# Projection of layer 0 of a gated DeltaNet and RG-LRU backbone: two of five blocks of sums of squares and transposes moved behind a tile's fifth block

## The chip, the cores and the metric

The kernel runs on one core of one Trainium2 chip. The metric is the device time of one execution in microseconds; smaller is better. Times within one execution come from one profiled execution.

## The reference

Two layers over a latent stream of 2048 tokens and a prefix of 256 context tokens, 1024 wide, everything in float32. Layer 0 mixes with a bidirectional gated DeltaNet, layer 1 with a bidirectional RG-LRU. What matters here is the head of layer 0:

```python
proj = h @ w_in                                   # 1024 x 6208
qkv, z, ab = jnp.split(proj, [GDN_QKV_W, GDN_QKV_W + GDN_V_W], axis=-1)
qkv = jax.nn.silu(short_conv(qkv, conv_w))        # 4 taps over time
q, k, v = jnp.split(qkv, [GDN_QK_W, 2 * GDN_QK_W], axis=-1)
q = l2norm(q) * (GDN_HEAD_DIM ** -0.5)            # per head of 128
k = l2norm(k)
g = -jnp.exp(a_log) * jax.nn.softplus(ab[..., 0, :] + dt_bias)
# later: decay = exp(cumsum(g)[c] - cumsum(g)[s]) for each chunk of tokens
```

There are 8 heads of q and k and 16 of v and z, 128 wide each.

## The kernel before

The program runs phases one after another: modulation, norm, gates, the projection of layer 0 (`phase_project_gdn`), the delta core, the output, and then the same kind of phases for layer 1. The change touches `phase_project_gdn` alone.

**Heads, tiles, blocks.** The phase loops over `NQ` = 8 heads h. A head has `NT` = 6 tiles of 128 output features, in the order Q, Z0, K, Z1, V0, V1. A tile is computed for 2304 tokens in `NB` = 5 blocks: one of 256 (block 0) and four of 512 tokens (blocks 1 to 4). Each block is 24 matmuls into its own PSUM bank, `pj_bank` (L565): 8 slices of the contraction by three products of high and low parts. A stage is one tile on each of the engines. Stage (h, j) of each engine is written out by hand in program order, and the engines meet only at semaphores. Head 0 is written out, heads 1 to 7 run in a hardware loop (SyncE and GpSimd have their last head written out too).

**What happens to a tile.** ScalarE copies each bank into `pj_raw` (`take`, L837; with SiLU for Z0 and Z1). For q, k and v VectorE convolves the row (`conv`, L947 and L951) into `pj_acc`, once all five blocks have been taken. There is one `pj_raw`, so the take of the next tile's block 0 waits for the convolution, or for the store of z. One stage later ScalarE applies SiLU into `pj_row` (L853).

- For q and k it squares the row into `pj_acc` (L857). TensorE sums the squares over the features with a matrix of ones (`norms`, L785), ScalarE takes the root of each block (`root`, L865), and VectorE takes the reciprocal of the row (L933) and multiplies (L935, `normalise`). SyncE stores the row (`store_fm`, L657).
- k and v are transposed by TensorE (`turn`, L801), 4 chunks of 128 tokens to a bank, copied by ScalarE into `pj_tm` (`collect`, L877) and stored (`store_tm`, L664).

So five of the six stages have a **group** on TensorE: Q the transposes of the last V1 (trV1), Z0 the sums for q, Z1 the sums for k, V0 the transposes of k (trK), V1 those of V0 (trV0). K has none. A group has five blocks, b = 0 to 4, in three PSUM banks, `aux[b % 3]`: block 3 may be written once ScalarE has read block 0, and block 4 once it has read block 1 (the semaphore `aux_read`). The group stands behind block 3 of the tile, so behind the fourth of its blocks:

```python
for blk in range(NB):
    pr.products(pe, h, j, blk, first)
    if blk != 3:
        continue
    ...
```

**Decays.** Beside that, each stage makes three chunks of decays, o = 0 to 2, with two buffers. SyncE loads a chunk (L677, L679), ScalarE takes the absolute difference (L885) and the exponential (L888), GpSimd multiplies (L751, L754, L755), and SyncE stores the result (L688) and, once that has landed, loads the chunk after next into the buffer. ScalarE's order in a stage is decay 0, take 0 and 1, SiLU and square of the row before, decay 1, take 2 and 3, the group's roots or copies, decay 2, take 4.

**SyncE's queue.** In a stage SyncE issues, in this order: the next tile's weights (L539), store_tm or the store of z (L650), the store and the load of the last stage's decay 2, those of decay 0, in K and V0 store_fm, which waits for `norm`, and those of decay 1. It issues nothing else meanwhile.

Of the kernel before, what the change touches and what calls it, by code (L numbers as in the profile page):

```python
# [42 lines left out]
NQ = 8  # L43
# [3 lines left out]
NB = len(BLKS)  # L47
# [535 lines left out]
def phase_project_gdn(nc, sem, T, io, dram, hi, lo):  # L583
# [3 lines left out]
    Q, Z0, K, Z1, V0, V1 = range(6)  # L587
# [6 lines left out]
    with ExitStack() as ctx:  # L594
# [27 lines left out]
            return h * sum(k in kinds for k in KINDS) + sum(k in kinds for k in KINDS[:j + 1])  # L622

        PT = NCH // NT

        def item(h, j, o):

# [11 lines left out]
        with nc.Block() as block:  # L639
# [133 lines left out]

            @block.tensor
            def _(pe):
                def norms(h, j):

                    pe.wait_ge(s["square"], nth(h, j, "qk"))
                    base = aux_before(h, "ssQ" if j == Q else "ssK")
                    for b, (at, n) in enumerate(BLKS):  # L780
                        if b >= 3:
                            pe.wait_ge(s["aux_read"], base + b - 2)
                        elif b == 0 and not (isinstance(h, int) and h == 0 and j == Q):
                            pe.wait_ge(s["aux_read"], base)
                        pe.matmul(aux[b % 3][:, 0:n], T["ones"][:], acc[:, at:at + n], start=True, stop=True  # L785
                                  ).then_inc(s["aux"], 1)

                def turn(h, j, use):

                    if j == K:  # L790
                        pe.wait_ge(s["norm"], nth(h, j, "qk"))
                    else:
                        pe.wait_ge(s["silu"], nth(h, j, "qkv"))
                    base = aux_before(h, use)
                    for b in range(NB):
                        if b >= 3:
                            pe.wait_ge(s["aux_read"], base + b - 2)
                        elif b == 0:
                            pe.wait_ge(s["aux_read"], base)
                        for c in range(TRB * b, min(TRB * b + TRB, NCH)):  # L800
                            i = pe.transpose(aux[b % 3][:, (c % TRB) * P:(c % TRB + 1) * P],  # L801
                                             act_row[:, c * P:(c + 1) * P], T["ident"][:])
                        i.then_inc(s["aux"], 1)

                def stage(h, j, first):
                    for blk in range(NB):
                        pr.products(pe, h, j, blk, first)
                        if blk != 3:
                            continue
                        if j == Q and not first:  # L810
                            turn(h - 1, V1, "trV1")
                        if j == Z0:
                            norms(h, Q)
                        if j == Z1:
                            norms(h, K)
                        if j == V0:
                            turn(h, K, "trK")
                        if j == V1:
                            turn(h, V0, "trV0")
                sweep(pe, stage)  # L820
                turn(NQ - 1, V1, "trV1")

            @block.scalar
            def _(act):
                def take(h, j, blk, first):

                    act.wait_ge(pr.s_mm, (h * NT + j) * NB + blk + 1)
                    if blk == 0:
                        if first:
                            act.wait_ge(s["pads"], 1)  # L830
                        elif KINDS[j - 1] == "z":
                            act.wait_ge(s["z_out"], 32 * nth(h, j - 1, "z"))
                        elif j == 0:
                            act.wait_ge(s["conv"], nth(h, j, "qkv") - 1)
                        else:
                            act.wait_ge(s["conv"], nth(h, j - 1, "qkv"))
                    act.activation(raw_row(raw, blk), pr.bank[blk][:, 0:BLKS[blk][1]],  # L837
                                   ACT.Silu if KINDS[j] == "z" else ACT.Copy).then_inc(pr.s_ev, 1)

                def silu(h, j):  # L840
                    act.wait_ge(s["conv"], nth(h, j, "qkv"))
                    if j == Q:
                        if not (isinstance(h, int) and h == 0):
                            act.wait_ge(s["aux"], aux_before(h, "ssQ"))
                    elif j == K:
                        act.wait_ge(s["fm_out"], 16 * nth(h, Q, "qk"))
                    elif j == V0:
                        act.wait_ge(s["fm_out"], 16 * nth(h, K, "qk"))
                        act.wait_ge(s["aux"], aux_before(h, "trK") + NB)
                    else:  # L850
                        act.wait_ge(s["aux"], aux_before(h, "trV0") + NB)
                    for dst, src in zip((act_row[:, 0:CTX], act_row[:, CTX:TOK]), sequences(acc)):
                        i = act.activation(dst, src, ACT.Silu)  # L853
                    i.then_inc(s["silu"], 1)
                    if KINDS[j] in "qk":
                        act.wait_ge(s["silu"], nth(h, j, "qkv"))
                        act.activation(acc[:, 0:TOK], act_row[:], ACT.Square).then_inc(s["square"], 1)  # L857

                def root(h, j):

                    base = aux_before(h, "ssQ" if j == Q else "ssK")
                    q = KINDS[j] == "q"
                    for b, (at, n) in enumerate(BLKS):
                        act.wait_ge(s["aux"], base + b + 1)
                        act.activation(acc[:, at:at + n], aux[b % 3][:, 0:n], ACT.Sqrt,  # L865
                                       bias=epsq[:] if q else T["eps"][:], scale=float(HD) if q else 1.0
                                       ).then_inc(s["aux_read"], 1)

                def collect(h, j, use):

                    base = aux_before(h, use)
                    if not (isinstance(h, int) and h == 0 and j == K):
                        act.wait_ge(s["tm_out"], 16 * nth(h, j, "kv") - 16)
                    for b in range(NB):
                        n = min(TRB, NCH - TRB * b)
                        act.wait_ge(s["aux"], base + b + 1)
                        act.activation(tm[:, TRB * b:TRB * b + n].rearrange("p c t -> p (c t)"),  # L877
                                       aux[b % 3][:, 0:n * P], ACT.Copy).then_inc(s["aux_read"], 1)

                def decay(h, j, o):  # L880
                    c, b, k, u = item(h, j, o)
                    act.wait_ge(d_load[b], u * 48 + 48)
                    for dr in range(2):
                        for v in range(2):
                            i = act.activation(E[b][:, dr, v], E[b][:, dr, v], ACT.Abs, scale=-1.0, bias=gi[b][:, dr, Q_CG, v:v + 1])  # L885
                    i.then_inc(s["d_abs"], 1)
                    act.wait_ge(s["d_abs"], k + 1)
                    act.activation(E[b][:], E[b][:], ACT.Exp, scale=-1.0).then_inc(s["d_exp"], 1)  # L888

                def stage(h, j, first):  # L890
                    decay(h, j, 0)
                    take(h, j, 0, first)
                    take(h, j, 1, first)
                    if j == Q and not first:
                        silu(h - 1, V1)
                    if j == Z0:
                        silu(h, Q)
                    if j == Z1:
                        silu(h, K)
                    if j == V1:  # L900
                        silu(h, V0)
                    decay(h, j, 1)
                    take(h, j, 2, first)
                    take(h, j, 3, first)
                    if j == Q and not first:
                        collect(h - 1, V1, "trV1")
                    if j == Z0:
                        root(h, Q)
                    if j == Z1:
                        root(h, K)  # L910
                    if j == V0:
                        collect(h, K, "trK")
                    if j == V1:
                        collect(h, V0, "trV0")
                    decay(h, j, 2)
                    take(h, j, 4, first)
                sweep(act, stage)
                silu(NQ - 1, V1)
                collect(NQ - 1, V1, "trV1")

            @block.vector
            def _(dve):
# [1348 lines left out]
```

## Time and profile before

| | |
|---|---|
| Median of 3 runs | 4664.9 us (4652.61 to 4669.88) |
| Profiled execution | 4631.9 us, span 4630.1 us |
| TensorE (PE) matmul, busy | 4124.7 us, 89% of the span |
| TensorE weight loads (PEld) | 3436.1 us, 74% |
| VectorE (DVE) | 2331.1 us, 50% |
| ScalarE (ACT) | 2280.2 us, 49% |
| GpSimd (POOL) | 2017.1 us, 44% |
| Projection of layer 0, first to last L565 matmul | from 244.1 to 1645.9 us of the span |

Busy times are sums over the span and overlap. Matmuls are pipelined, and their ends are modelled. "[2.98 <-ACT pj_acc L865]" behind a row means that the engine stood idle for 2.98 us before it, and that the wait ended with the named work. SPq is SyncE's DMA queue; the row of a DMA lasts as long as its issue, not as long as the transfer. The projection's stages start where the first matmul of a tile's block 0 stands on TensorE.

### The profile page before, as it was taken

What the parts mean: (1) busy time and instruction counts of PE and PEld (TensorE: products, weight loads), DVE (VectorE), ACT (ScalarE), POOL (GpSimd) and SP (SyncE); (2) the same over time, 40 slices, a digit from 0 to 9 for tenths busy, and PEclk for the clock granted to TensorE, in tenths of its full rate; (3) what the DMA queues carried; (4) which work ended last, traced back from release to release, by engine and by line L of the source; (5) the groups of instructions that cost most, each with busy time, mean ns of one, the idle gap of its engine ahead of it and who ended that gap; (6) DMA issues with size and microseconds to landing.
All of it is one profiled execution on the core that took longest, in us unless ns stands there. A gap on an engine that the chain in (4) does not pass through costs nothing. (4 is left out here: it accounts for less than half of the span.)

```text
span 4630.1 us, 85462 instructions
## 1 busy us (share of the span) xinstructions
PE 4124.7 (89%) x30756; PEld 3436.1 (74%) x30756; DVE 2331.1 (50%) x2947; ACT 2280.2 (49%) x4473; POOL 2017.1 (44%) x1524
## 2 busy tenths in 40 slices
PE   6689999999999969999999999995999599977869
PEld 2377777777777758888888888884888488866657
DVE  3234444433433446666666666655554423338853
ACT  4245555555555546666666666652111511138832
POOL 2255455455555547666666666653111412100022
PEclk8799999999999989999999999997999699988889
DMA  6245545544544556666666666645444322254244
GB/s 227 91 122 150 150 142 151 152 139 144 151 144 143 158 170 197 182 193 190 192 179 193 188 184 188 183 137 204 177 181 154 100 100 104 110 225 180 80 141 136
DMA packets 775776, 733.27 MB, mean 158 GB/s; under 512 B 111808, under 2 KB 702656, under 8 KB 758272
## 3 DMA queue, kind: packets, MB, share of 16 engines
q1 hardware_dynamic: 775456, 728.67, 50.6%
q8 instruction: 242, 3.96, 0.3%
q14 instruction: 78, 0.64, 0.0%
HBM read 483.12 MB, written 245.33 MB: 157 GB/s over the span
## 5 line engine op out<-in xcount | busy, mean ns | idle before, releaser
L565 PE MATMUL pj_bank<-h_hi,pj_whi 128*128 128x512 f32 (+1 forms) x1920 | 725.7, 378 | 23.3 <-POOL pj_wlo L551 20.1
L565 PE MATMUL pj_bank<-h_lo,pj_whi 128*128 128x512 f32 (+1 forms) x1920 | 711.8, 371 | 0.0
L565 PE MATMUL pj_bank<-h_hi,pj_wlo 128*128 128x512 f32 (+1 forms) x1920 | 710.6, 370 | 0.0
L1345 ACT ACTIVATE dc_R<-dc_psE 128x256 f16<-128x256 f32 x864 | 285.8, 381 | 435.6 <-PE dc_psE L1222 435.3
L1419 DVE TENSOR_TENSOR dc_Y<-dc_psY,dc_pick 128x256 f16<-128x256 f32 x864 | 325.9, 419 | 336.5 <-PE dc_psY L1208 336.5
L751 POOL TENSOR_TENSOR pj_BD<-pj_E,pj_gi 128x512 f32<-128x512 f32 x144 | 189.4, 1316 | 651.7 <-ACT pj_E L888 651.7
L565 PEld LDWEIGHTS pj_bank<-h_hi,pj_whi 128*128 128x128 f32 x1920 | 367.4, 191 | 91.8 <-POOL pj_wlo L551 20.6
L565 PEld LDWEIGHTS pj_bank<-h_lo,pj_whi 128*128 128x128 f32 x1920 | 366.1, 191 | 66.2 <-issue 6.8
L565 PEld LDWEIGHTS pj_bank<-h_hi,pj_wlo 128*128 128x128 f32 x1920 | 365.3, 190 | 61.5
L1137 POOL TENSOR_TENSOR dc_A<-dc_Lhi,dc_id 128x512 f16<-128x512 f16 x144 | 166.4, 1155 | 483.1 <-ACT dc_Lhi L1336 483.1
L933 DVE RECIPROCAL pj_acc<-pj_acc 128x2304 f32<-128x2304 f32 x16 | 232.9, 14553 | 263.1 <-ACT pj_acc L865 263.1
L885 ACT ACTIVATE pj_E<-pj_E,pj_gi 128x128 f32<-128x128 f32 x576 | 184.2, 395 | 282.6 <-DMA pj_gi<-scratch_gates 282.4
L947 DVE TENSOR_SCALAR pj_acc<-pj_raw,pj_conv_w 128x2307 f32<-128x2307 f32 x32 | 48.8, 1526 | 534.5 <-ACT pj_raw L837 534.5
L1349 ACT ACTIVATE dc_X<-dc_psE 128x256 f16<-128x256 f32 x864 | 287.9, 396 | 0.0
L837 ACT ACTIVATE pj_raw<-pj_bank 128x512 f32<-128x512 f32 (+1 forms) x240 | 126.2, 554 | 325.4 <-PE pj_bank L565 164.5
L951 DVE SCALAR_TENSOR_TENSOR pj_acc<-pj_raw,pj_conv_w,pj_acc 128x2307 f32<-128x2307 f32 x96 | 267.3, 2785 | 13.7 <-DVE pj_acc L951 2.3
L2112 POOL TENSOR_TENSOR ol_lo<-ol_mix,ol_hi 128x1024 fp32r<-128x1024 f32 x16 | 45.8, 2865 | 488.0 <-ACT ol_hi L2125 488.0
L565 PE MATMUL pl_bank<-h_hi,pl_whi 128*128 128x512 f32 (+1 forms) x640 | 236.5, 369 | 17.0 <-POOL pl_wlo L551 17.0
L1208 PE MATMUL dc_psY<-dc_R,dc_A 128*128 128x64 f16 x3456 | 187.8, 195 | 64.9 <-issue 46.2
L1279 PE MATMUL dc_psO<-dc_S,dc_qd 128*128 128x128 f32 x1152 | 243.8, 293 | 0.0
L565 PE MATMUL pl_bank<-h_lo,pl_whi 128*128 128x512 f32 (+1 forms) x640 | 236.3, 369 | 0.0
L565 PE MATMUL pl_bank<-h_hi,pl_wlo 128*128 128x512 f32 (+1 forms) x640 | 236.0, 369 | 0.0
(267 smaller groups left out, 10433.8 us busy)
## 6 DMA issues: line engine op xcount, KB each, us to landing
dc_dd<-scratch_decays SPq DMA_DIRECT2D x288, 256.0 KB, 5.5
dc_tm<-scratch_tm SPq DMA_DIRECT2D x288, 192.0 KB, 2.4
pj_E<-scratch_cgrow SPq DMA_DIRECT2D x288, 128.0 KB, 3.7
scratch_decays<-pj_E SPq DMA_DIRECT2D x144, 256.0 KB, 3.7
scratch_decays<-pj_BD SPq DMA_DIRECT2D x144, 256.0 KB, 3.7
dc_fm<-scratch_fm SPq DMA_DIRECT2D x288, 128.0 KB, 3.2
dc_egr<-scratch_egrow SPq DMA_DIRECT2D x288, 128.0 KB, 3.6
scratch_o<-dc_ob SPq DMA_DIRECT2D x288, 128.0 KB, 3.3
```

What stands on the lines that cost most here:

```text
L565: i = pe.matmul(self.bank[blk][:, 0:n], l[b][:, k, :], r[:, k, at:at + n], start=(m == 0), stop=(m == 3 * KT - 1))
L751: pool.tensor_tensor(BD[b][:], E[b][:], gi[b][:, :, Q_BETA, :].unsqueeze(3).broadcast_to(C4), ALU.mult).then_inc(s["d_scaled"], 1)
L837: act.activation(raw_row(raw, blk), pr.bank[blk][:, 0:BLKS[blk][1]], ACT.Silu if KINDS[j] == "z" else ACT.Copy).then_inc(pr.s_ev, 1)
L885: i = act.activation(E[b][:, dr, v], E[b][:, dr, v], ACT.Abs, scale=-1.0, bias=gi[b][:, dr, Q_CG, v:v + 1])
L933: dve.reciprocal(acc[:, 0:TOK], acc[:, 0:TOK]).then_inc(s["recip"], 1)
L951: dve.scalar_tensor_tensor(acc[:], raw[:, m:m + CONV], tap(m), acc[:], ALU.mult, ALU.add).then_inc(s[f"conv{m}"] if m < 3 else s["conv"], 1)
L1137: pool.tensor_tensor(flat(A[q][p]), flat(Lhi[p]), id16[:], ALU.add).then_inc(s_A[p], 1)
L1208: m = pe.matmul(quart(bY[p])[:, c * 64:(c + 1) * 64], comb(A[q][p], c), cols(R[q][p], c, l, True), start=True, stop=True)
L1279: pe.matmul(comb(bO, c), comb(qd[q][p], c), comb(S[q][p], c), start=True, stop=False)
L1345: act.activation(all_cols(R[q][p], l, True), split4(quart(bE[p]), l), ACT.Copy).then_inc(eR[p], 1)
L1349: act.activation(all_cols(X[q][p], l, False), split4(quart(bE[p], 1), l), ACT.Copy).then_inc(eX[p], 1)
L1419: dve.tensor_tensor(all_cols(Y[l - 1][p], l, True), split4(quart(bY[p]), l), split4(pick[:, l - 1].rearrange("p c t -> p (c t)"), l), ALU. ...
```

## The change

A group is cut in two: its blocks 0, 1 and 2 (part 0) stay behind block 3 of the tile, and its blocks 3 and 4 (part 1) go behind block 4, on TensorE (`norms`, `turn`) and on ScalarE (`root`, `collect`). On ScalarE decay 2 and take 4 stand between the two parts. The waits for the row (`square`, `norm`, `silu`) and for the store of `pj_tm` stay with part 0. The last group of the phase runs both parts one after the other.

```diff
+        PARTS = (range(3), range(3, NB))
...
-                def norms(h, j):
-
-                    pe.wait_ge(s["square"], nth(h, j, "qk"))
+                def norms(h, j, part):
+
+                    if part == 0:
+                        pe.wait_ge(s["square"], nth(h, j, "qk"))
                     base = aux_before(h, "ssQ" if j == Q else "ssK")
-                    for b, (at, n) in enumerate(BLKS):
+                    for b in PARTS[part]:
+                        at, n = BLKS[b]
                         if b >= 3:
                             pe.wait_ge(s["aux_read"], base + b - 2)
...
                 def stage(h, j, first):
                     for blk in range(NB):
                         pr.products(pe, h, j, blk, first)
-                        if blk != 3:
+                        if blk < 3:
                             continue
                         if j == Q and not first:
-                            turn(h - 1, V1, "trV1")
+                            turn(h - 1, V1, "trV1", blk - 3)
                         if j == Z0:
-                            norms(h, Q)
+                            norms(h, Q, blk - 3)
...
                     take(h, j, 2, first)
                     take(h, j, 3, first)
-                    if j == Q and not first:
-                        collect(h - 1, V1, "trV1")
-                    if j == Z0:
-                        root(h, Q)
...
+                    beside(h, j, first, 0)
                     decay(h, j, 2)
                     take(h, j, 4, first)
+                    beside(h, j, first, 1)
```

`beside` is the same list of calls of `root` and `collect` by stage, with the part handed on.

TensorE, first head, stage Z0 from its last matmuls of block 3 on (`pj_aux` is the group, `pj_bank` the tile), before:

```order
L565 MATMUL pj_bank<-h_hi,pj_wlo_1234 128x512
L785 MATMUL pj_aux<-pj_acc,ones 128x256
L785 MATMUL pj_aux<-pj_acc,ones 128x512 x4
L565 MATMUL pj_bank<-h_hi,pj_whi 128x512
L565 MATMUL pj_bank<-h_lo,pj_whi 128x512
```

and with the change, block 4 shortened:

```order
L565 MATMUL pj_bank<-h_hi,pj_wlo_1234 128x512
L788 MATMUL pj_aux<-pj_acc,ones 128x256
L788 MATMUL pj_aux<-pj_acc,ones 128x512 x2
L565 MATMUL pj_bank<-h_hi,pj_whi 128x512
...
L565 MATMUL pj_bank<-h_hi,pj_wlo_1234 128x512
L788 MATMUL pj_aux<-pj_acc,ones 128x512 x2
L565 MATMUL pj_bank<-h_hi,pj_whi 128x256
```

All 24 matmuls of block 4 stand between the third sum and the fourth now, and the last two sums are the last thing before the next tile.

ScalarE, the same stage from decay 1 on to the next tile's first decay (L837 is a take, L865 a root, L885 and L888 a decay), before:

```order
L885 ACTIVATE pj_E<-pj_E,pj_gi 128x128 x4
L888 ACT_TABLE_LOAD
L888 ACTIVATE pj_E<-pj_E 128x512
L837 ACT_TABLE_LOAD
L837 ACTIVATE pj_raw<-pj_bank 128x512 x2
L865 ACT_TABLE_LOAD
L865 ACTIVATE pj_acc<-pj_aux,pj_epsq 128x256
L865 ACTIVATE pj_acc<-pj_aux,pj_epsq 128x512 x4
...
L837 ACT_TABLE_LOAD
L837 ACTIVATE pj_raw<-pj_bank 128x512
L885 ACTIVATE pj_E<-pj_E,pj_gi 128x128 x4
```

and with the change, from the first roots on (L841 is the take, L870 the root, L890 and L893 the decay):

```order
L870 ACT_TABLE_LOAD
L870 ACTIVATE pj_acc<-pj_aux,pj_epsq 128x256
L870 ACTIVATE pj_acc<-pj_aux,pj_epsq 128x512 x2
L890 ACTIVATE pj_E<-pj_E,pj_gi 128x128 x4
L893 ACT_TABLE_LOAD
L893 ACTIVATE pj_E<-pj_E 128x512
L841 ACT_TABLE_LOAD
L841 ACTIVATE pj_raw<-pj_bank 128x512
L870 ACT_TABLE_LOAD
L870 ACTIVATE pj_acc<-pj_aux,pj_epsq 128x512 x2
L890 ACTIVATE pj_E<-pj_E,pj_gi 128x128 x4
```

The last two roots stand behind decay 2 and take 4, with a table load of their own. In the stages with transposes the copies move in the same way, without a table load. The order on VectorE, GpSimd and SyncE is as before.

## Rows read from the trace of the kernel before

**Rows 1.** Windows: the whole projection, and stage K of the third head
```profile
core 0: us, PE busy (x) PEld busy (x) DVE busy (x) ACT busy (x) POOL busy (x), PEclk, DMA share, GB/s
244.10:1645.90 1401.80, 1330.31 (x6334) 1091.05 (x6334) 597.12 (x156) 772.64 (x1372) 735.08 (x526) 0.98 0.49 144
656.90:681.60 24.70, 24.70 (x121) 20.92 (x121) 14.80 (x2) 9.70 (x21) 13.68 (x12) 1.00 0.66 198
```
**Rows 2.** Waits of the projection: total us, times, longest us
```profile
ACT pj_E L885 <- DMA pj_gi<-scratch_gates: 264.2, 73, 7.1
...
PE pj_aux L785 <- ACT pj_acc L865: 41.6, 16, 4.1
...
PE pj_aux L801 <- ACT pj_tm L877: 26.7, 14, 4.0
```
**Rows 3.** Timeline of TensorE, stages Z0 and V0: start us, us, operation
```profile
644.37 2.31 PE L785 MATMUL pj_aux<-pj_acc,ones 128*128 128x256 f32 x6
649.66 1.98 PE L785 MATMUL pj_aux<-pj_acc,ones 128*128 128x512 f32 x4 [2.98 <-ACT pj_acc L865]
651.08 0.80 PE L565 MATMUL pj_bank<-h_hi,pj_whi 128*128 128x512 f32 x1
...
733.68 2.27 PE L801 MATMUL pj_aux<-ident,pj_row 128*128 128x128 f32 x18
```
**Rows 4.** Timeline of SyncE's queue and ScalarE, from V0 to the next Z0
```profile
731.94 0.39 SPq L657 DMA_DIRECT2D scratch_fm<-pj_row  x1
...
743.15 0.40 SPq L664 DMA_DIRECT2D scratch_tm<-pj_tm  x1
...
758.33 1.28 ACT L885 ACTIVATE pj_E<-pj_E,pj_gi 128x128 f32<-128x128 f32 x4 [1.39 <-DMA pj_gi<-scratch_gates]
...
774.78 0.39 SPq L664 DMA_DIRECT2D scratch_tm<-pj_tm  x1
...
788.35 1.28 ACT L885 ACTIVATE pj_E<-pj_E,pj_gi 128x128 f32<-128x128 f32 x4 [3.38 <-DMA pj_gi<-scratch_gates]
...
801.00 0.40 SPq L664 DMA_DIRECT2D scratch_tm<-pj_tm  x1
...
816.18 1.28 ACT L885 ACTIVATE pj_E<-pj_E,pj_gi 128x128 f32<-128x128 f32 x4 [0.38 <-DMA pj_gi<-scratch_gates]
```
**Rows 5.** Timeline of ScalarE, stage Z0 of the third head
```profile
642.22 1.26 ACT L885 ACTIVATE pj_E<-pj_E,pj_gi 128x128 f32<-128x128 f32 x4
...
647.84 1.28 ACT L865 ACT_TABLE_LOAD   x1
649.13 2.38 ACT L865 ACTIVATE pj_acc<-pj_aux,pj_epsq 128x256 f32<-128x256 f32 x4
...
652.26 1.27 ACT L885 ACTIVATE pj_E<-pj_E,pj_gi 128x128 f32<-128x128 f32 x4
...
655.50 1.28 ACT L837 ACT_TABLE_LOAD   x1
```
**Rows 6.** Groups of VectorE in the projection: busy us, mean ns, idle before
```profile
L933 DVE RECIPROCAL pj_acc<-pj_acc 128x2304 f32<-128x2304 f32 x16 | 232.9, 14553 | 263.1 <-ACT pj_acc L865 263.1
L935 DVE TENSOR_TENSOR pj_row<-pj_row,pj_acc 128x2304 f32<-128x2304 f32 x16 | 57.4, 3588 | 0.6
```
**Rows 7.** Timeline of SyncE's queue and ScalarE, from K to Z1, third head
```profile
674.48 0.40 SPq L657 DMA_DIRECT2D scratch_fm<-pj_row  x1
...
688.89 1.28 ACT L885 ACTIVATE pj_E<-pj_E,pj_gi 128x128 f32<-128x128 f32 x4 [6.48 <-DMA pj_gi<-scratch_gates]
...
696.04 2.14 ACT L857 ACTIVATE pj_acc<-pj_row 128x2304 f32<-128x2304 f32 x1
```
**Rows 8.** Timeline of VectorE: the multiplication of k, first and last of eight heads
```profile
373.88 3.22 DVE L935 TENSOR_TENSOR pj_row<-pj_row,pj_acc 128x2304 f32<-128x2304 f32 x1
...
1601.74 3.52 DVE L935 TENSOR_TENSOR pj_row<-pj_row,pj_acc 128x2304 f32<-128x2304 f32 x1
```
**Rows 9.** SyncE's queue and ScalarE, sixth head: store_fm(K), second decay of next Z0
```profile
1257.44 0.39 SPq L657 DMA_DIRECT2D scratch_fm<-pj_row  x1
...
1344.68 1.26 ACT L885 ACTIVATE pj_E<-pj_E,pj_gi 128x128 f32<-128x128 f32 x4
```

More of the change, by code:

```diff
@@ L786, in norms, with turn @@
                                   ).then_inc(s["aux"], 1)
-                def turn(h, j, use):
-                    if j == K:
+                def turn(h, j, use, part):
+                    if part == 0 and j == K:
                         pe.wait_ge(s["norm"], nth(h, j, "qk"))
-                    else:
+                    elif part == 0:
                         pe.wait_ge(s["silu"], nth(h, j, "qkv"))
                     base = aux_before(h, use)
-                    for b in range(NB):
+                    for b in PARTS[part]:
                         if b >= 3:
@@ L807, in stage @@
                         pr.products(pe, h, j, blk, first)
-                        if blk != 3:
+                        if blk < 3:
                             continue
                         if j == Q and not first:
-                            turn(h - 1, V1, "trV1")
+                            turn(h - 1, V1, "trV1", blk - 3)
                         if j == Z0:
-                            norms(h, Q)
+                            norms(h, Q, blk - 3)
                         if j == Z1:
-                            norms(h, K)
+                            norms(h, K, blk - 3)
                         if j == V0:
-                            turn(h, K, "trK")
+                            turn(h, K, "trK", blk - 3)
                         if j == V1:
-                            turn(h, V0, "trV0")
+                            turn(h, V0, "trV0", blk - 3)
                 sweep(pe, stage)
-                turn(NQ - 1, V1, "trV1")
+                for part in range(2):
+                    turn(NQ - 1, V1, "trV1", part)
             @block.scalar
@@ L857, in silu, with root @@
                         act.activation(acc[:, 0:TOK], act_row[:], ACT.Square).then_inc(s["square"], 1)
-                def root(h, j):
+                def root(h, j, part):
                     base = aux_before(h, "ssQ" if j == Q else "ssK")
                     q = KINDS[j] == "q"
-                    for b, (at, n) in enumerate(BLKS):
+                    for b in PARTS[part]:
+                        at, n = BLKS[b]
                         act.wait_ge(s["aux"], base + b + 1)
@@ L867, in root, with collect @@
                                        ).then_inc(s["aux_read"], 1)
-                def collect(h, j, use):
+                def collect(h, j, use, part):
                     base = aux_before(h, use)
-                    if not (isinstance(h, int) and h == 0 and j == K):
+                    if part == 0 and not (isinstance(h, int) and h == 0 and j == K):
                         act.wait_ge(s["tm_out"], 16 * nth(h, j, "kv") - 16)
-                    for b in range(NB):
+                    for b in PARTS[part]:
                         n = min(TRB, NCH - TRB * b)
@@ L888, in decay, with beside @@
                     act.activation(E[b][:], E[b][:], ACT.Exp, scale=-1.0).then_inc(s["d_exp"], 1)
+                def beside(h, j, first, part):
+                    if j == Q and not first:
+                        collect(h - 1, V1, "trV1", part)
+                    if j == Z0:
+                        root(h, Q, part)
+                    if j == Z1:
+                        root(h, K, part)
+                    if j == V0:
+                        collect(h, K, "trK", part)
+                    if j == V1:
+                        collect(h, V0, "trV0", part)
                 def stage(h, j, first):
@@ L904, in stage @@
                     take(h, j, 3, first)
-                    if j == Q and not first:
-                        collect(h - 1, V1, "trV1")
-                    if j == Z0:
-                        root(h, Q)
[L909 to L914, printed above, removed]
+                    beside(h, j, first, 0)
                     decay(h, j, 2)
                     take(h, j, 4, first)
+                    beside(h, j, first, 1)
                 sweep(act, stage)
                 silu(NQ - 1, V1)
-                collect(NQ - 1, V1, "trV1")
+                for part in range(2):
+                    collect(NQ - 1, V1, "trV1", part)
             @block.vector
```

## Prediction

> **What bounds the kernel now.** I read the table of windows first, then the waits of the projection, then the timelines of TensorE, SyncE's queue with ScalarE, and VectorE. A measurement of this kernel tells about 0.5% (23 us) from no change; the three runs lie 17 us apart.
>
> The change touches the projection of layer 0 alone. There TensorE is busy 1330 of 1402 us at a granted clock of 0.98 [rows 1], so it looks like the bound. Its waits there are nearly all for ScalarE in one place: 41.6 us before the sums of squares and 26.7 us before the transposes, 68.3 us together [rows 2]. One such group: three blocks of sums go out at 644.37, the fourth waits 2.98 us until ScalarE has read the first, since there are three `aux` banks, and block 4 of the tile starts at 651.08, behind it [rows 3]. That wait is what the change takes away.
>
> But ScalarE is not late because it is busy: it waits 264 us for the decays' loads [rows 2]. So a second chain must be walked before the 68 us are booked. I write N for the moment at which VectorE has normalised k (the end of L935); store_fm(K) and the trK transposes wait for it. I go from one N to the next.
>
> **Link 1, store_fm(K) to the second decay of Z0, without TensorE.** store_fm(K) goes out at 731.94. The decays' loads stand behind it on SyncE, and each step waits for the one before: store_tm 743.15, second decay of V1 on ScalarE 758.33, store_tm 774.78, second decay of Q 788.35, store_tm 801.00, second decay of Z0 816.18 [rows 4]. The three decays come 15.18, 13.57 and 15.18 us after their store_tm. The whole link is 816.18 - 731.94 = 84.2 us.
>
> **Link 2, second decay to normalised row, as it is.** Decay and exp, a table load, takes 2 and 3 and another load last from 642.22 to 649.13, 6.9 us; the five roots end at 652.3 [rows 5], 10.1 us in all. Then come the reciprocal, 14.55, and the multiplication, 3.59 [rows 6]: 18.2 with the gap.
>
> **The change, part by part.**
> - TensorE: the same matmuls. Between part 0 and part 1 now lies block 4, 24 matmuls or some 5.5 us (4.5 such blocks are K's 24.7 us [rows 1]). By then ScalarE's first roots or copies are done or nearly so; up to all of the 68.3 us go. Alone this is -68 us.
> - ScalarE, roots: those of blocks 3 and 4 stand behind decay 2 and take 4 now. From the second decay: 6.9 as before, three roots 1.75, decay 2 with the load of its exp 3.24 (652.26 to 655.50), a load 1.28, take 4 0.6, **one table load more** 1.28, two roots 1.3: 16.4 where rows 5 have 10.1. Each normalised row comes **6.3 us later**. There are 16 such loads.
> - The price of a load: the root starts at 649.13 and its load has ended at 647.84 + 1.28 = 649.12 [rows 5], so I take 1.28. The Trainium skill (ScalarE: Activation LUTs, What ACT_TABLE_LOAD costs) adds a drain of about 1.38 us to every switch; by that the sum would be 16 x 1.38 = 22 us worse. The row shows no drain.
> - ScalarE, copies: two of five come after take 4. They push back the next tile's first decay, which mostly waits for its load anyway, and store_tm by about 1 us; store_tm has room, as it stood 11.2 us behind store_fm [rows 4]. I take 0, and 1 us a head as the other bound.
> - SyncE: the order of the DMAs stays, but store_fm waits for the later row, and behind it stand a store of decays and the load for the next tile's first decay. Nearest row: store_fm(Q) at 674.48 to that decay on ScalarE at 688.89, 14.4 us [rows 7]. In it the store waited some 2 us for its own decay; now it goes out at once, into a queue full of store_fm's packets. Bounds: 12.4 if those 2 us come back, 15.2 as behind a store_tm [rows 4]. I take 14.4.
> - From that decay to the squares' end: 696.04 + 2.14 - 688.89 = 9.3 [rows 7], of which 0.9 was a wait for a convolution that will be over: 8.4.
> - VectorE and POOL: the same work, covered by TensorE's 24.7 to 28 us per tile. It is thin in K: by the sum below the norm of q ends 25.7 us into K, and the convolution of k can start at 25.3 at best.
>
> **The new loop.** N to the second decay of Z0, 0.2 + 84.2; to the normalised q, 16.4 + 18.2; store_fm, 0.2; the first decay of Z1, 14.4; the squares of k, 8.4 + 0.1; the next N, 16.4 + 18.2. The sum is **176.7 us per head**. Before, seven heads take from 377.1 to 1605.3, 175.5 each [rows 8]. So seven cost 7 x 1.2 = +8.4.
>
> TensorE inside it: a head without waits is six tiles of 24.7, two groups of sums at 3.8 (6.71 less the wait [rows 3]) and three of transposes at 2.0 [rows 3], 161.6 us. The other 15 must show as waits. Its turn for trK is 3.5 blocks, 19.2 us, into V0, and N comes at 25.7: **6.5 us before the first transposes of V0**. The squares of k are ready 24.0 us into Z1: **4.8 us there**. Z0 waits some 3.3 for the second root at its part 1, and Q has the rest.
>
> Ends: head 0 has no link 1 before it. The norm of q is about as much later as K begins earlier, so its squares of k are ready when they were, and of the two 6.3 only one counts, less some 1.8 that the roots waited for TensorE there: N at 381.6 for 377.1, **+4.5**, an estimate. After the last N TensorE has 7.6 + 26.7 = 34.3 us of work left against 1645.9 - 1605.3 = 40.6, **-6.3**.
>
> Sum: 8.4 + 4.5 - 6.3 = **+7 us** on the profiled execution's 4631.9, which is 33 us below the median of the runs, 4664.9. On that median: **4672**.
>
> Bounds. With 13.57 in place of both 15.18 link 1 is 81.0, a head 173.5 and the sum 7 x -2.0 - 1.8 = -16; with the 2 us given back at both store_fm, 169.5 and -44. The longest of the seven links 1 is 87.2 [rows 9]: a head of 179.7 and 7 x 4.2 - 1.8 = +28.
>
> **The rivals.**
> 1. *TensorE's waits simply go.* For it: it is busy 95% of the phase, ScalarE not much over half. It gives 68 us, and up to 27 more if the clock goes from 0.98 to 1.00 (2% of 1330): 4597 to 4570; half of it, if trK is seldom late, 4631. Against it: link 1 holds no TensorE, and N, which came 13.3 us into V0, comes 6.3 later by its own roots and meets a V0 that starts as much earlier as Z1's wait was. The Trainium skill (TensorE: Matmul & The Clock Gate) warns against idle gaps of the array, which speaks for this rival only if no longer gaps take their place. Chance 0.13.
> 2. *The later rows cost more than the wait gives: slower.* Place: store_fm behind the norm on SyncE, and the decays' loads behind that, twice a head. It decides from a link 1 of 86.5 us, or from 1.6 us more behind each store_fm; either makes a head 179.0 and the sum +23. Price: +28 at 87.2, and 14 more if each store_fm also holds the queue 1 us longer: 4693 to 4707. For it: the same 87.2. Against it: the long links may hold slack given by TensorE's waits. Chance 0.27.
> 3. *A little faster*: link 1 at its shortest and the queue soon free behind store_fm, -24 to -44: 4641 to 4621. Chance 0.05.
>
> **How the numbers follow.** Within 0.5% (4642 to 4688): 0.55. Rival 2 is slower, 0.27; rivals 1 and 3 are faster, 0.18. The likeliest is 4672. The range 4634 to 4706 leaves out most of rivals 1 and 3 and the far end of 2, some 0.2.
>
> **What the profile after would show.** Right: TensorE's waits at part 1 for copies nearly gone; 32 table loads for roots; a wait of 5 to 8 us of the trK transposes for VectorE's multiplication in nearly every V0, and one of 3 to 6 us of the sums for the squares in Z1; a head of 175 to 178 us. Wrong: if trK hardly waits, or a head is under 172 us, the second chain had slack that I did not see, and rival 1 holds. A decay well over 15 us behind its store_fm would be rival 2.

## The result, and the profile after

| | before | after |
|---|---|---|
| Median | 4658.8 us (4 runs, 4649.1 to 4669.9) | 4618.8 us (4 runs, 4612.9 to 4624.0) |
| Profiled execution | 4631.9 us | 4624.0 us |
| Ratio after/before | | 0.9914, 95% interval 0.9889 to 0.9938 |

The kernel is 0.9% faster, 40 us. I had forecast 4672 us, no change, and a range that began at 4634: too slow, and with too narrow a range. In a later group, five runs beside 23 of the kernel before, the same change came to 0.9954 (0.994 to 0.9968), with medians 17 us apart. The sign holds in both; the size is open between 17 and 40 us.

The two profiled executions lie only 8 us apart. The windows show why: the projection is 23.2 us shorter, and the delta core, whose code is the same, 10.9 us longer.

The windows of the kernel after, projection (first to last matmul of its tiles) and delta core:

```profile
core 0: us, PE busy (x) PEld busy (x) DVE busy (x) ACT busy (x) POOL busy (x), PEclk, DMA share, GB/s
247.40:1626.00 1378.60, 1320.50 (x6328) 1091.94 (x6329) 597.33 (x156) 791.66 (x1386) 776.18 (x526) 0.98 0.50 147
1655.90:3112.80 1456.90, 1366.26 (x17999) 1221.19 (x18000) 920.05 (x2168) 901.80 (x2447) 956.27 (x864) 0.97 0.63 184
```

and the window of the delta core in the kernel before:

```profile
1675.20:3121.20 1446.00, 1357.41 (x18000) 1214.72 (x18000) 920.83 (x2170) 901.25 (x2447) 955.95 (x864) 0.98 0.64 185
```

So the projection went from 1401.8 [rows 1] to 1378.6. Its waits after (total us, times, longest):

```profile
ACT pj_E L890 <- DMA pj_gi<-scratch_gates: 366.3, 91, 18.8
...
PE pj_aux L804 <- DVE pj_row L945: 31.0, 8, 5.1
...
PE pj_aux L788 <- ACT pj_acc L861: 12.0, 7, 2.3
PE pj_aux L788 <- ACT pj_acc L870: 9.6, 5, 2.6
```

Against [rows 2]: the 26.7 us before the transposes are gone, and the 41.6 before the sums are 9.6. Two waits are new, and they are those that the prediction named: the transposes of k wait for VectorE's multiplication in each of the eight heads, and the sums for the squares in seven cases. ScalarE waits 83 us more for the decays' loads: the 366.3 hold the 18.8 us before the first load of the phase, and the window of [rows 2], 264.2, begins just behind that wait (18.3 us there). The wait went from TensorE to the engine that had been late all along for another reason.

The groups of VectorE and of the table load in the projection after:

```profile
L943 DVE RECIPROCAL pj_acc<-pj_acc 128x2304 f32<-128x2304 f32 x16 | 232.8, 14553 | 370.8 <-ACT pj_acc L870 370.8
...
L945 DVE TENSOR_TENSOR pj_row<-pj_row,pj_acc 128x2304 f32<-128x2304 f32 x16 | 45.1, 2822 | 0.6
```

```profile
L870 ACT ACT_TABLE_LOAD x32 | 41.1, 1283 | 0.6
```

There are 32 table loads for roots, as forecast. The multiplication takes 2.82 us where [rows 6] had 3.59, which I had not forecast.

### The profile page after: what moved, and what is told of

The parts are those of the page before. It is cut to its first block and busy times, and to the rows that moved or that the text cites. A ratio compares the mean times of both kernels' runs of the same rounds, so it can differ in the third digit from the quotient of the medians.

```text
span 4622.2 us, 85478 instructions
## 1 busy us (share of the span) xinstructions
PE 4124.6 (89%) x30756; PEld 3443.0 (74%) x30756; DVE 2333.6 (50%) x2947; ACT 2300.4 (50%) x4489; POOL 2054.6 (44%) x1524
## 5 line engine op out<-in xcount | busy, mean ns | idle before, releaser
L752 POOL TENSOR_TENSOR pj_BD<-pj_E,pj_gi 128x512 f32<-128x512 f32 x144 | 180.0, 1250 | 587.4 <-ACT pj_E L893 587.4
L890 ACT ACTIVATE pj_E<-pj_E,pj_gi 128x128 f32<-128x128 f32 x576 | 184.0, 392 | 366.4 <-DMA pj_gi<-scratch_gates 366.3
L961 DVE SCALAR_TENSOR_TENSOR pj_acc<-pj_raw,pj_conv_w,pj_acc 128x2307 f32<-128x2307 f32 x96 | 279.5, 2911 | 13.7 <-DVE pj_acc L961 2.3
L755 POOL TENSOR_TENSOR pj_BD<-pj_BD,pj_strict 128x512 f32<-128x512 f32 x144 | 232.7, 1616 | 11.3
```

Of the source, the lines that this page charges most:

```text
L752: pool.tensor_tensor(BD[b][:], E[b][:], gi[b][:, :, Q_BETA, :].unsqueeze(3).broadcast_to(C4), ALU.mult).then_inc(s["d_scaled"], 1)
L755: pool.tensor_tensor(BD[b][:], BD[b][:], strict[:].unsqueeze(2).broadcast_to(C4), ALU.mult)
L961: dve.scalar_tensor_tensor(acc[:], raw[:, m:m + CONV], tap(m), acc[:], ALU.mult, ALU.add).then_inc(s[f"conv{m}"] if m < 3 else s["conv"], 1)
```

## The experiments

They ran in three groups of four, in the order of the table, the first two groups on one chip and the third on another; each ratio is to the kernel before in the same group (medians there 4641.0, 4642.4 and 4639.8 us, from 23, 26 and 9 runs). "Head" is the distance from the K stage of the first head to that of the last, divided by seven, from the profile; "link 1" is the mean over seven heads of store_fm(K) to the second decay of the next Z0. Head, projection and link 1 come from one profiled execution each, the ratio from all executions.

| run | ratio (95%) | projection us | head us | link 1 us |
|---|---|---|---|---|
| before, again | 1.0017 (1.0003 to 1.0031) | 1393.8 | 174.5 | 83.9 |
| the change, again | 0.9954 (0.994 to 0.9968) | 1383.2 | 173.6 | 84.3 |
| sums alone | 0.9953 (0.9938 to 0.9968) | 1392.0 | 174.9 | 85.2 |
| copies alone | 1.0004 (0.9993 to 1.0015) | 1403.4 | 176.0 | 84.2 |
| sums, half a block | 0.9908 (0.9881 to 0.9935) | 1376.8 | 173.2 | 87.2 |
| both, half a block | 0.9945 (0.9924 to 0.9966) | 1376.0 | 173.3 | 86.0 |
| change, store_fm late | 0.9954 (0.9939 to 0.997) | 1379.5 | 173.2 | 77.7 |
| before, store_fm late | 1.0027 (1.0009 to 1.0044) | 1414.5 | 177.4 | 77.4 |
| before, early E | 0.9954 (0.9941 to 0.9968) | 1373.9 | 171.6 | 82.5 |
| change, early E | 0.9891 (0.9874 to 0.9909) | 1348.1 | 169.3 | 80.3 |
| sums half a block, early E | 0.9839 (0.9817 to 0.9861) | 1320.1 | 165.1 | 81.4 |
| both half a block, early E | 0.9831 (0.9817 to 0.9844) | 1321.8 | 165.5 | 81.7 |

### Both kernels again

> The kernel before, once more, for the spread of its parts. In its profile at hand the projection (first to last matmul of the tiles) lasts 1401.7 us and the delta core (first dc_psG to last dc_psO) 1446.0; with the change 1378.6 and 1456.9. If the delta core varies from run to run with the same code, it lasts anything from 1446 to some 1470 here, and the projection 1395 to 1410. If the projection is what varies, it lasts 1420 or more and the delta core 1446. Ratio 1.000 within 0.3%.

> The change as it is, once more, for the spread. Ratio 0.991 within 0.3%; projection 1375 to 1382 us if it is steady, delta core anything from 1446 to 1470 if that varies.

The kernel before against itself came out at 1.0017, and its interval leaves out 1: a ratio of this kind can be trusted to some 0.2%, whatever its interval says. The change came out at 0.9954, where I had expected 0.991 within 0.3%. The profile of the kernel before, again:

```profile
248.80:1642.60 1393.80, 1324.06 (x6334) 1087.38 (x6334) 597.50 (x156) 772.81 (x1372) 730.33 (x526) 0.98 0.49 145
1672.20:3133.80 1461.60, 1368.95 (x17999) 1222.83 (x18000) 920.74 (x2170) 901.68 (x2447) 956.00 (x864) 0.97 0.63 183
```

The delta core is 1461.6 with the same code that took 1446.0, the projection 1393.8 where it took 1401.8. Both vary by 8 to 16 us between executions, so one pair of profiles can't size a change of 20 to 40 us. Over both pairs the head goes from 175.6 and 174.5 to 173.1 and 173.6, 1.7 us on the mean. The projection is 23.2 and 10.6 us shorter, some 60% of what the medians moved (40 and 17 us); where the rest was gained the profiles do not show.

### One part of the change at a time

The expectations set two theories against each other. In theory A a loop that runs through the decays sets the time of a head; in theory B the time comes out of TensorE's own waits, each by itself. The kernels hold a second table, `WHOLE = (range(NB), range(0))`, which puts all five blocks into part 0:

```diff
 def turn(h, j, use, part):          # and collect: sums alone
-    for b in PARTS[part]:
+    for b in WHOLE[part]:
```

> Only the sums of squares and their roots are cut in two; transposes and copies stay whole behind block 3. Theory A (the head is set by the loop norm, store_fm, decays, norm): the norms are as late as with the whole change, so the head is 173 to 176 us, the wait of the trK transposes for VectorE stays some 5 us per head, and the whole run is at 0.99 to 1.00 of before. Theory B (the time came out of TensorE's own waits, each by itself): 41.6 us fewer less the new wait at trK, and the transposes' waits of 26.7 us stay; a ratio of 0.995, so worse than the whole change by its copies' 27 us (0.6%).

```diff
 def norms(h, j, part):              # and root: copies alone
-    for b in PARTS[part]:
+    for b in WHOLE[part]:
```

> Only the transposes and their copies are cut in two; the sums and roots stay whole behind block 3, so no norm is later and no table load is added. Theory A: the loop through the norms is some 12 us shorter, no wait at trK, and a head is then TensorE's own 161.6 us plus the two waits at the sums with the slow clock behind them (5 to 7 us), 167 to 169; seven heads save some 50 us against before, and it beats the whole change: ratio 0.987 to 0.990. Theory B: only the transposes' 26.7 us go, ratio 0.994, worse than the whole change.

Sums alone came out as the whole change by the ratio, and copies alone as no change. In its profile sums alone has a head of 174.9, no shorter than before; that execution, at 4636.6 us, was the slowest of its six (median 4622.2). Copies alone missed both expectations, 0.987 to 0.990 by theory A and 0.994 by theory B. That speaks for theory A in that the transposes' waits are worth nothing, and against the sum it had made: with no norm late, I had expected 167 to 169 us, and a head is 176.0. The waits of TensorE with copies alone show where it went:

```profile
PE pj_aux L789 <- ACT pj_acc L871: 70.8, 16, 9.2
...
PE pj_aux L805 <- ACT pj_row L858: 12.2, 1, 12.2
```

Q fell from 30.4 to 26.7 us on the mean of the middle heads, and Z0 grew from 32.2 to 38.6. TensorE gives up its waits in V1 and Q, comes to Z0's sums earlier, and waits there 70.8 us where it had waited 41.6, until ScalarE has had its second decay. Link 1 is 84.2 us in this kernel and 83.9 before: these waits of TensorE do not change it.

So there is a loop **in the kernel before too**, which I had not written down: link 1 83.9, second decay of Z0 to K 15.4, K 24.7, Z1 32.7, V0 up to store_fm 17.6, together 174.3, with a head of 174.5. That the sum is a head proves nothing: the terms are stretches that follow one another from one store_fm(K) to the next. What it tells is where the waits lie. Only the sums' waits, in Z0 and Z1, lie outside link 1. They are what the change could take out; the 26.7 us of the transposes lie beside link 1, and that they are worth nothing is what copies alone shows.

### Part 1 in the middle of block 4

To have the wait covered and the norm not late, the fourth and fifth sums go between the two halves of block 4, and ScalarE takes all five roots before decay 2 as it did before:

```diff
 for blk in range(NB):
-    pr.products(pe, h, j, blk, first)
+    pr.products(pe, h, j, blk, first, range(KT // 2) if blk == 4 else range(KT))
     ...                             # part blk - 3 of the group
+pr.products(pe, h, j, 4, False, range(KT // 2, KT))
...
 beside(h, j, first, 0)
+beside(h, j, first, 1)
 decay(h, j, 2)
 take(h, j, 4, first)
-beside(h, j, first, 1)
```

> Sums cut in two, but part 1 stands in the middle of block 4 (after 12 of its 24 matmuls), and ScalarE takes all five roots before decay 2 as in the kernel before: no later norm, no further table load. Transposes and copies whole behind block 3 as before. Theory A (before, the head is the loop: store_fm(K) to the second decay of Z0, 84 us without TensorE; then Z0's sums, K, Z1's sums with block 4 behind their wait; then V0 up to store_fm): the sums' waits of some 2.7 us each leave the loop and nothing is added, a head falls from 175 to 169 to 171 us, trK does not wait for VectorE; ratio 0.988 to 0.993, better than the change. Theory B (what counts is that TensorE has a whole block to cover ScalarE): half a block is 2.7 us and covers most of 2.7 us, so about the same, 0.995.

> As e5, and the transposes' part 1 in the middle of block 4 as well. Theory A: the transposes' waits lie beside the 84 us link that holds no TensorE, so this gains nothing over e5 (within 0.2%), as cutting the copies alone gained nothing. Theory B: 25 us more come out, 0.5% better than e5.

The ratio, 0.9908, fell into the band of theory A, but not by its reason. A head is 173.2, not 169 to 171, as long as with the change. The sums' waits are 9.9 us in all and trK does not wait for the norm, yet the transposes wait 46.1 us, and link 1 has grown to 87.2:

```profile
PE pj_aux L807 <- ACT pj_tm L886: 46.1, 15, 6.1
...
PE pj_aux L791 <- ACT pj_acc L874: 9.9, 10, 2.1
```

The projection is 6 us shorter than in the profile of the change on that chip; the rest of what parts these two executions is the delta core, 1443 us in this one and 1459 in that one. Whether that holds for the other executions behind the ratio is not shown. With the transposes in halves as well the head is 173.3 again, and Z0 34.2 for 28.9; that its ratio is 0.004 above the other's, at a projection as short and intervals that overlap, I leave open. So a head is 173.1 to 173.6 us in the profiles of the change and of both half blocks, which leave TensorE different waits. That the chain of decays holds it there is argued here, and tested two sections on.

### store_fm one step later

```diff
+finish(h, j, 1, last)               # store and load of decay 1
 if j == K:
     store_fm(h, Q)
 if j == V0:
     store_fm(h, K)
-finish(h, j, 1, last)
```

> The change, with SyncE's store_fm moved behind the store and load of the stage's decay 1 (one step later in its queue), so that no decay waits for the norm. Theory A (in the changed kernel the loop goes through norm, store_fm and the decays' loads behind it): the first decay of Z1 comes 5 to 8 us into Z1 instead of 12.6 to 13, the squares of k at 16.5 to 17.5 instead of 21, TensorE's wait in Z1 goes, and the wait at trK falls from 5 to 2 to 4; a head of 167 to 171 us, ratio 0.985 to 0.992. Rival: store_fm's 1152 KB delay the decays' loads wherever they stand, and the decays are late all the same: within 0.2% of the change.

> The kernel before with the same move of store_fm. There the norm is ready (13.3 us into K and V0) before SyncE comes to store_fm (17.5), so nothing waits in that place: theory A expects 1.000 within 0.3%, with the first decays of Z1 and V1 some 1 to 2 us earlier at most. If it gains as much as e7, then not the wait for the norm but the packets of store_fm ahead of the decays were the cost.

Theory A failed here in the changed kernel; the rival in the expectation, within 0.2% of the change, came true (0.9954 both). In the kernel before theory A held only in that nothing was gained. With the change the first decay of Z1 does come after 7.7 to 10.7 us (heads 1 to 6) instead of 12.5 to 13.1 in the first profile of the change and 11.5 to 13.4 in the second, but the squares of k end only about 1.5 us earlier and the roots behind them take 17.7 for 16.2; the wait of the trK transposes rose from 4.4 to 4.9 us each, where 2 to 4 were expected. From N to the second decay of Z0 it is 6.8 + 77.7 = 84.5 us where the change has 0.2 + 84.0: the decays' wait for the norm was removed, and the same 84 us remained. Removing that wait gained nothing. Whether store_fm's packets delay the loads wherever they stand, as the rival says, or the decays' chain holds the head by itself, these two runs cannot tell. In the kernel before the first decay of Z1 came some 4 us sooner, and Z1 still grew by 1.5 us and the head by 2.9.

### The chain of decays by itself

GpSimd applies E's mask before BD's, SyncE stores E when it is ready, and the next load into that buffer waits for E's store alone:

```diff
-pool.tensor_tensor(BD, BD, strict, ALU.mult)
-pool.tensor_tensor(E, E, incl, ALU.mult).then_inc(d_done, 1)
+pool.tensor_tensor(E, E, incl, ALU.mult).then_inc(d_edone, 1)
+pool.tensor_tensor(BD, BD, strict, ALU.mult).then_inc(d_done, 1)
...
-sp.wait_ge(d_done, k + 1)           # then both stores on d_out[b]
+sp.wait_ge(d_edone, k + 1)          # store E, on d_out[b]
+sp.wait_ge(d_done, k + 1)           # store BD, on d_bd[b]
```

> The kernel before, with each chunk of decays stored in two steps: GpSimd multiplies E before BD, SyncE stores E at once and BD when it is ready, and the load of the chunk after next waits for E's store alone (GpSimd waits for BD's). Each link from a decay to the next load into its buffer gets about 1.8 us shorter (one GpSimd pass of 1.2, one issue of 0.6). TensorE, the sums and the norms are untouched. Theory A (the head of the kernel before is the loop with 84 us of decays and loads between store_fm(K) and the second decay of Z0): the link falls from 84 to 78 to 80, a head from 174 to 168 to 171, ratio 0.988 to 0.993. Theory B (the head is TensorE's work and its waits for ScalarE, decays beside it): 1.000 within 0.2%.

> The change, with the same early store of E. Theory A: link 1 shortens by some 5 us here as well, a head from 173 to 167 to 169, ratio to before 0.984 to 0.989; trK still waits for VectorE. Theory B: as the change, 0.995.

> Sums with part 1 in the middle of block 4 (e5), with the early store of E. Theory A: both parts of the loop are shortened, a head of 163 to 167 us, near TensorE's own 161.6; ratio 0.977 to 0.985, the best so far. Theory B: as e5, 0.991.

> Sums and transposes with part 1 in the middle of block 4 (e6), with the early store of E. With link 1 shorter the transposes' waits may lie on the path: theory A expects it within 0.3% of e11, 0.2% better if they do. Theory B: as e6, 0.9945.

This shows the chain of decays on the path. Nothing of TensorE's order is touched, and the kernel before gets 0.46% faster, where theory B had 1.000 within 0.2%; theory A's 0.988 to 0.993 was too much. Its head falls from 174.5 to 171.6: link 1 gave 1.4 us rather than 4 to 6, and V0 up to store_fm 1.4 more (17.6 to 16.2). Three things moved together, the order of the masks, the store of E, and what the load waits for; no run parts them. ScalarE's wait for the decays' loads in that kernel, which was 264 us [rows 2] (the row holds the 18.6 us before the phase's first load, so 146 are like those 264):

```profile
ACT pj_E L891 <- DMA pj_gi<-scratch_gates: 164.6, 49, 18.6
```

On top of it the change takes the head to 169.3 (0.9891), and half a block for the sums to 165.1 (0.9839). Theory A had 0.984 to 0.989 and 0.977 to 0.985, theory B 0.995 and 0.991. In the profiles half a block for the sums is worth 1.3 us a head without the early store (174.5 to 173.2), and 6.5 with it (171.6 to 165.1). The ratios say this less clearly. With half a block for both, the two edits gave 0.55% and 0.46% apart and 1.69% together, which is clear of the intervals; for the sums' half block it is 0.92% and 0.46% against 1.61%, and for the change 0.46% and 0.46% against 1.09%, both within them.

The window of the projection with the sums' half block and the early E shows TensorE busy 1303.7 of 1320.0 us, at a full clock:

```profile
246.70:1566.70 1320.00, 1303.68 (x6334) 1077.29 (x6334) 601.75 (x156) 768.77 (x1372) 761.26 (x526) 1.00 0.53 153
```

That is 73.8 us shorter than in the profile of before, again; 20.4 of them are TensorE's own busy time (1324.1 there, at a granted clock of 0.98), the rest its waits.

The two kernels with half a block and early E have medians of 4556.9 and 4558.9 us, against 4639.8 for the kernel before beside them and 4590.1 for the change with early E. The transposes' halves are worth nothing measurable (0.9831 and 0.9839).

## Why the prediction was wrong

**The loop: 3.6 us too long, and not held together as I had it.** Its terms in the profile after, means over heads 1 to 7:

| term of the sum | forecast | measured |
|---|---|---|
| link 1, with the step to store_fm | 0.2 + 84.2 | 0.2 + 84.0 |
| second decay of Z0 to the reciprocal | 16.4 | 16.2 |
| normalised q | 18.2 | 17.4 |
| store_fm(Q) to the first decay of Z1 | 0.2 + 14.4 | 0.2 + 13.2 |
| squares of k | 8.4 + 0.1 | 8.4 |
| to the reciprocal | 16.4 | 16.2 |
| normalised k | 18.2 | 17.4 |
| head | 176.7 | 173.1 |

The links can be read off the third head, as [rows 4] for before. SyncE's queue and ScalarE in the profile after:

```profile
721.34 0.39 SPq L658 DMA_DIRECT2D scratch_fm<-pj_row  x1
...
731.49 0.40 SPq L665 DMA_DIRECT2D scratch_tm<-pj_tm  x1
...
762.11 0.39 SPq L665 DMA_DIRECT2D scratch_tm<-pj_tm  x1
...
777.14 1.28 ACT L890 ACTIVATE pj_E<-pj_E,pj_gi 128x128 f32<-128x128 f32 x4 [5.12 <-DMA pj_gi<-scratch_gates]
...
790.72 0.40 SPq L665 DMA_DIRECT2D scratch_tm<-pj_tm  x1
...
806.40 1.28 ACT L890 ACTIVATE pj_E<-pj_E,pj_gi 128x128 f32<-128x128 f32 x4 [3.26 <-DMA pj_gi<-scratch_gates]
```

806.40 - 721.34 is 85.1 us, for 84.2 in [rows 4]. Two terms of the sum were mis-sized:

1. *"the reciprocal, 14.55, and the multiplication, 3.59"*: the multiplication is 2.82 now (see below), 0.8 us in each of two norms, 1.6 a head.
2. *"Bounds: 12.4 if those 2 us come back ... I take 14.4"*: 1.2 of the 2 us did come back: the next load's last DMA follows store_fm after 7.3 to 8.7 us in 15 of 16 cases, where it was 8.8 to 9.9 in 14. The reason that I had given, that the store goes out at once, is seen in few: it follows store_fm after 0.5 to 1.0 us in 5 of 16, and after 2.1 in ten, where it was 2.3 to 2.7. What holds it there is open. The third head is one of the five, with its load 7.65 us behind store_fm:

```profile
666.86 0.40 SPq L658 DMA_DIRECT2D scratch_fm<-pj_row  x1
667.87 1.72 SPq L689 DMA_DIRECT2D scratch_decays<-pj_E  x1
...
674.51 0.34 SPq L680 DMA_DIRECT2D pj_gi<-scratch_gates  x1
```

Two roots' legs 0.2 us shorter and link 1 0.2 shorter make the rest. 7 x 3.6 is 25 of the 30 us between the forecast +7 and the measured -23 of the projection in that profile.

The step behind the sum is not borne out either. The prediction says "store_fm waits for the later row, and behind it stand a store of decays and the load", and makes that the path on which a later norm costs time. With store_fm one step later in the changed kernel the decays no longer waited for the norm, and the head was 173.2 us, with 84.5 from N to the second decay of Z0, as before that edit. The terms of my loop follow one another through a whole head, so they had to add up to it whatever held it; their fit is no proof of the path. What the runs show in its place is that shortening the decays' chain alone shortens a head (174.5 to 171.6, and 173.6 to 169.3 with the change). Which step of that chain sets its pace stays open.

**The ends: 5 us too long.** I had N of the first head at +4.5 and it came 2.5 us earlier, 130.5 us after the projection's start for 133.0. I had put that "its squares of k are ready when they were". They were ready 6.4 us sooner, 97.2 us after the projection's start for 103.6: the first decay of Z1 stands at 336.24, 10.3 us after store_fm at 325.91 (12.3 before), and the squares end 8.4 us behind it (13.0 before). After the last N it was 36.3 us for 40.6, -4.3 where I had -6.3, since the taking of part 1 and V1 last 36.3 and not 34.3.

**What held.** All the new waits came, in their places, but smaller than I had said: N reached V0 after 22.4 to 24.8 us in heads 0 to 7 (forecast 25.7), and the transposes of k waited for it in all eight, 3.9 us on the mean (5 to 8); the squares of k ended 20.9 to 21.5 us into Z1 in the middle heads (24.0), and the sums waited 1.7 us on the mean (3 to 6); Q was 26.7 us. A head was forecast to 2%, and 2% of a head are 3.6 us, more than the 2.4 by which the change shortened it in this pair of profiles. The bounds I had set for single terms reached down to 169.5 us a head, yet I gave rival 3, which is what they add up to, a chance of 0.05 and let the range end inside it.

**The rivals.** Rival 3 comes nearest, by half of its reason: the load behind store_fm came 1.2 of the 2 us sooner, but link 1 was 84.0 and not at its shortest, 81.0. The shorter multiplication was in no rival. Its price was -24 to -44; the medians moved -40 in the first result and -17 in the second group. Rival 1 is refuted by the copies alone: 26.7 us of waits went, and nothing was gained. Rival 2 did not come: no head was longer than 176.7 us in either profile of the change. But its place was real: with the later norm, store_fm goes out later too, 23.9 us into V0 where it was 17.6 in the first group's profile of before. Its second condition is summed wrongly: 1.6 us more behind each of two store_fm makes 3.2, a head of 179.9 and +29, not 179.0 and +23.

**The price of a table load.** The load ended and the root began at once, as in [rows 5], now in 16 further places:

```profile
646.03 1.28 ACT L870 ACT_TABLE_LOAD   x1
647.33 1.27 ACT L870 ACTIVATE pj_acc<-pj_aux,pj_epsq 128x512 f32<-128x512 f32 x2
```

646.03 + 1.28 = 647.31. ScalarE's busy time rose from 2280.2 to 2300.4 us, by 20.2; 16 x 1.28 is 20.5. The drain of some 1.38 us that the Trainium skill adds (ScalarE: Activation LUTs, What ACT_TABLE_LOAD costs) is not there, and the measurement decides.

## What to carry to other kernels

When an engine waits for another, ask first what that one waits for. Here TensorE waited 68 us for ScalarE, ScalarE 264 us for loads, and the loads for stores and GpSimd passes; shortening that chain by itself gained as much as the change did beside the kernel before (0.46% each), and with half a block for both groups in place of the change the two together gained 1.69%. Walk the chain through the kernel *before* as well and see which waits lie in it: the loop I had left out there would have told that the transposes' waits may be worth nothing and the sums' something. But stretches that follow one another always add up to the period; whether one really waits for the other takes an edit that removes that wait alone, as moving store_fm did. And where two loops come out within 2% of each other, the sign is not forecast: the range has to hold both.

## What the runs showed of the hardware

**Which of two engines is slowed depends on which began.** GpSimd's and VectorE's operations with two SBUF operands hold each other up. The kernel before ran all 16 multiplications (L935) beside GpSimd's split of the weights, which was running already in 15 cases: 3.2 to 4.7 us. In the sixteenth VectorE was first: 2.56 us, and the split took 4.64 instead of 2.4. With the change the multiplication comes later and meets GpSimd's decays. In 14 of 16 cases a pass of GpSimd is running already, but such a pass lasts 1.04 to 1.17 us, and the multiplication is held up only by what is left of it: it takes 2.56 to 3.4 us. The GpSimd pass behind it now pays, and GpSimd's busy time in the projection rose from 735.1 [rows 1] to 776.2 us. VectorE, then GpSimd in the profile after:

```profile
718.55 2.56 DVE L945 TENSOR_TENSOR pj_row<-pj_row,pj_acc 128x2304 f32<-128x2304 f32 x1
```

```profile
718.69 3.44 POOL L755 TENSOR_TENSOR pj_BD<-pj_BD,pj_strict 128x512 f32<-128x512 f32 x1
```

That pass (L755) takes 1.2 us in all 85 cases of the 144 in which VectorE does nothing beside it, and also in the 19 beside the reciprocal alone, which has one operand. Where it began first, as here 0.2 us ahead of the multiplication of q, it takes 1.17, and the multiplication 3.39:

```profile
663.02 1.17 POOL L755 TENSOR_TENSOR pj_BD<-pj_BD,pj_strict 128x512 f32<-128x512 f32 x1
664.15 3.48 POOL L756 TENSOR_TENSOR pj_E<-pj_E,pj_incl 128x512 f32<-128x512 f32 x1
```

```profile
663.22 3.39 DVE L945 TENSOR_TENSOR pj_row<-pj_row,pj_acc 128x2304 f32<-128x2304 f32 x1
```

The second one gets next to nothing done until the first has ended: the pass of 718.69 ends at 722.13, 1.02 us behind the multiplication's end at 721.11, and needs 1.17 alone.

The Trainium skill states the sharing (GPSIMD Engine Reference, 1. Specifications: contention with VectorE instructions that have two SBUF inputs); the rows agree, and show besides that the one that began first keeps its pace. This is read from where the two overlap; no run changed that alone.

**The same code varies by 1%.** The delta core took 1443 to 1462 us in the profiles of kernels that differ only ahead of it. What sets it was not tried.
